# A 32-expert layer on one core: the down weights move from the sync engine's DMA queue to ScalarE's

## The reference, cut to what matters

```python
def hier_moe(h, w_group, w_router, w_gate, w_up, w_down):
    ...                      # 4 groups x 8 experts; a token takes the group with the largest
    ...                      # probability and in it the two experts with the largest
    def expert_block(args):
        xb, e = args
        return (jax.nn.silu(xb @ w_gate[e]) * (xb @ w_up[e])) @ w_down[e]
    ...                      # every token gets the weighted sum of its two experts' rows
```

## Time and profile before

| | us |
|---|---|
| median of 3 runs (1653.45 to 1655.84) | 1654.09 |
| the profiled execution's own time | 1657.84 |
| its span, first to last instruction | 1656.1 |
| TensorE busy in the span | 1534.6 (93%) |
| expert layer in the span, from about 255 to 942 | 687 |

### The profile page before, as it was taken

The page is one execution under the profiler, slowest core; times in us unless marked ns, Lnnn a source line. Parts: engine busy times, 40 slices in busy tenths (PEclk is TensorE's granted clock), DMA queues, the critical chain, the costliest instruction groups (busy, mean ns, idle before and its releaser), DMA issues.

```text
span 1656.1 us, 22332 instructions
## 1 busy us (share of the span) xinstructions
PE 1534.6 (93%) x9534; PEld 1079.2 (65%) x9534; DVE 565.9 (34%) x982; ACT 330.4 (20%) x530; POOL 23.0 (1%) x31
## 2 busy tenths in 40 slices
PE   6997689999999999999999789999789999899996
PEld 4784475444444444444444479999677767799996
DVE  4747632111111110111111175555435263355553
ACT  2202221111111111111111132222200041244441
POOL 0002000000000000000000000000100000000000
PEclk9897888999999999999999999999989999999997
DMA  9870457999999999999999968777386500345440
GB/s 371 342 256 1 174 240 311 428 432 434 433 432 433 431 433 428 432 432 433 433 433 432 376 233 291 261 271 261 104 336 231 201 1 25 129 153 203 173 157 25
DMA packets 124504, 480.32 MB, mean 290 GB/s; under 512 B 6316, under 2 KB 53673, under 8 KB 108081
## 3 DMA queue, kind: packets, MB, share of 16 engines
q1 hardware_dynamic: 120896, 476.99, 71.8%
q10 hardware_dynamic: 3121, 1.18, 0.3%
q0 software_dynamic: 448, 1.59, 0.3%
HBM read 478.68 MB, written 1.06 MB: 290 GB/s over the span
## 4 chain that ended last, share of the span: by engine, by line
PE 71%; DMA 20%; DVE 5%; ACT 2%; ACTq 1%; issue 1%; SPq 0%; DVEq 0%
DMA arena<-in_w_up_dram 18%; PE psum L870 16%; PE psum L1196 16%; PE psum L1123 13%; PE psum L1217 8%; PE psum L1142 5%; PE psum L1107 2%; PE psum L1089 2%; PE psum L886 1%; DMA arena<-in_w_in_dram 1%; PE psum L969 1%; PE psum L1010 1%; PE psum L1021 1%; PE psum L895 1%; PE psum L904 1%
## 5 line engine op out<-in xcount | busy, mean ns | idle before, releaser
L1123 PE MATMUL psum<-arena,squares 128*64 128x384 f32 x2048 | 337.9, 487 | 19.4 <-DMA arena<-in_w_up_dram 14.6
L1123 PEld LDWEIGHTS psum<-arena,squares 128*64 128x64 f32 x2048 | 145.9, 137 | 213.5 <-issue 181.5
L1720 DVE TENSOR_TENSOR mixT<-mixT,psum 128x384 f32<-128x384 f32 x32 | 26.4, 827 | 489.2 <-PE psum L1123 489.2
L870 PE MATMUL psum<-hT,arena 128*128 128x256 f32 (+1 forms) x784 | 174.5, 385 | 11.8 <-DMA arena<-in_w_in_dram 10.3
L870 PEld LDWEIGHTS psum<-hT,arena 128*128 128x128 f32 (+1 forms) x784 | 150.3, 193 | 34.2 <-DMA arena<-in_w_in_dram 10.7
L1142 PE MATMUL psum<-arena,small 128*64 128x512 f32 x768 | 171.9, 597 | 0.0
L1142 PEld LDWEIGHTS psum<-arena,small 128*64 128x64 f32 x768 | 52.4, 137 | 95.9 <-issue 94.0
L1196 PE MATMUL psum<-ff_x_hi,ff_w_hi 128*128 128x256 f32 x704 | 106.4, 293 | 8.8 <-ACT ff_x_hi L678 8.8
L1765 DVE TENSOR_TENSOR ff_w_lo<-arena,ff_w_hi 128x2048 fp32r<-128x2048 f32 x44 | 100.8, 2291 | 16.8 <-ACT ff_w_hi L770 15.3
L1196 PEld LDWEIGHTS psum<-ff_x_hi,ff_w_hi 128*128 128x128 f32 x704 | 93.7, 192 | 12.5 <-issue 9.5
L1382 DVE SCALAR_TENSOR_TENSOR mod_acc<-arena,cond,mod_acc 128x512 f32<-128x512 f32 x133 | 100.0, 752 | 4.7
(11 more groups left out here) (265 smaller groups left out, 1404.2 us busy)
## 6 DMA issues: line engine op xcount, KB each, us to landing
arena<-in_w_gate_dram SPq DMA_DIRECT2D x32, 3072.0 KB, 31.6
arena<-in_w_up_dram SPq DMA_DIRECT2D x32, 3072.0 KB, 33.9
arena<-in_w_down_dram SPq DMA_DIRECT2D x32, 3072.0 KB, 31.6
arena<-in_ffn_w_in_dram SPq DMA_DIRECT2D x44, 1024.0 KB, 7.1
arena<-in_w_ada_dram SPq DMA_DIRECT2D x18, 2048.0 KB, 11.7
arena<-in_w_mod_dram SPq DMA_DIRECT2D x12, 2048.0 KB, 16.2
arena<-in_w_in_dram SPq DMA_DIRECT2D x11, 2048.0 KB, 13.8
arena<-in_ffn_w_out_dram SPq DMA_DIRECT2D x22, 1024.0 KB, 4.8
```

The costliest lines, as they stand in the source:

```text
L870: last = pe.matmul(dst, lhsT=lhs[i], rhs=rhs[i], start=(i == 0), stop=(i == n - 1))
L1123: last = pe.matmul(b[64 * half:64 * half + 64, 0:HALF_E], lhsT=xeT[:, k, u * SLOTS:(u + 1) * SLOTS], rhs=w[:, k, half * HALF_E:(half + 1) ...
L1720: nc.vector.tensor_tensor(hidden.rearrange("q (c p) -> q p c", c=3), gate_act.rearrange("q (p c) -> q p c", c=3), bank[5][:, 0:HALF_E].rea ...
```

## The change

The loop of SyncE no longer waits for `down_done` and no longer requests the down block. ScalarE requests it, on its own queue, right behind its copy of expert e-2's result to `y_e`; its loop is one pair shorter, and the last pair, which has nothing to load behind it, is written out. The down blocks of experts 0 and 1 and the second pass stay with SyncE.

```diff
-            def load_expert(u, e, done):
+            def load_expert(u, e, done, with_down=True):
                 sp.wait_ge(sem("gate_done"), done)
                 load_gate(u, e)
                 sp.wait_ge(sem("gate_up_done"), done)
                 load_up(u, e)
-                sp.wait_ge(sem("down_done"), done)
-                load_down(u, e)
+                if with_down:
+                    sp.wait_ge(sem("down_done"), done)
+                    load_down(u, e)
...
-                    load_expert(u, it * 2 + u, it * 2 + u - 1)
+                    load_expert(u, it * 2 + u, it * 2 + u - 1, with_down=False)
...
+            def next_down(u, e):
+                _, _, down = expert_w(u)
+                act.dma_start(down.rearrange("p (h c) n -> p h c n", h=2),
+                              ins["w_down"][0][bass.ds(e, 1)].rearrange("a (h p c) n -> p (a h) c n", h=2, p=P))\
+                   .then_inc(sem(f"down_full{u}"), 16)
+
             pair_in(1)
-            with act.Fori(0, N_EXPERTS // 2) as it:
+            with act.Fori(0, N_EXPERTS // 2 - 1) as it:
                 for u in range(2):
                     expert_steps(u, it * 2 + u + 1, it + 2)
+                    next_down(u, it * 2 + u + 2)
+            for u in range(2):
+                expert_steps(u, N_EXPERTS - 1 + u, N_EXPERTS // 2 + 1)
```

## The result

The changed kernel takes 1661.01 us (median of 5 runs, 1659.19 to 1662.61) against 1654.09 us: a ratio of 1.0045, 95% interval 1.003 to 1.006. The prediction had 1660.7 us. When it was run again beside the first experiments it took 1661.28 us, a ratio of 1.0043 (1.0029 to 1.0057) to the kernel before. Single executions of some versions were slower at a lower clock than the rest of the same kernel; the ratios leave them out, the medians of the two versions with four transfers for each down block do not.

What follows compares the result with a forecast made beforehand. DMA transfers were taken to bound the expert layer, narrowly ahead of TensorE. Requesters cost 0, arrival order 6.6 us, added to the median 1654.09 for 1660.7 us; range 1652.5 to 1667.

Steps and rivals of the forecast that it cites:

- What bounds the kernel: Expert layer: DMA transfers at 432 GB/s, 43.68 us a pair against TensorE's 40.77; last byte kept at 926.6.
- SyncE and ScalarE at no cost: Expert loop: moving 30 requests of 0.38 us from SyncE to ScalarE costs 0 us, hidden in waits and idle time.
- Packets in turn: DMA engines take one packet from each queue in turn, whatever its size; down blocks get a third of the rate.
- R: Gate and up packets still to come when expert 30's down block is through; taken as 4, end 943.2, 6.6 us late.
- The equal counts and the third of the bytes: Sign in the expert stretch: as many packets of q10 (down blocks) as of q1, with a third of the bytes.
- its bounds: End of the layer: between 3.4 us late (R = 7.5) and 10.2 us late (R = 0).
- the same formula: End of the layer: at or after the later of 946.8 - 0.91 R and 936.6 + 0.455 R.
- a mixing out of step: Sign: if q10, the down blocks' queue, runs dry between blocks, the queues do not mix as written out.
- Waits from 520 on, about 29 us in total: TensorE in the expert layer: waits on even experts' down blocks, starting near 520, about 29 instead of 19 us.
- What follows the layer shifts along: Behind the expert layer: everything moves with its later end; nothing from 972 to 1186 gives time back.
- rival 3: Expert stretch: mixing two streams lowers the DMA rate; one percent less adds 6.5 us, 1667.2 us; chance 0.11.
- no effect: Whole kernel: down packets served in request order or blocks still landing in order of use; 1654.1 us; chance 0.14.
- two queues fill gaps: Stretch from 267 to 926: second queue fills idle moments, each percent 6.5 us; 1647.6 at 2%; chance 0.15.

Runs made afterwards that it cites:

- the run with 90 requests on ScalarE: Changed kernel with SyncE's loop taken out, ScalarE requesting gate, up and down blocks of experts 2 to 31; layer 675.3 us, ratio 1.0015 to the kernel before.
- the run with the short tail: Kernel before, with expert 31's gather for a pair that does not exist cut from 32 matmuls to 4; layer 674.6 us, ratio 1.0009.

## Why the prediction was right, and where it was not

- *What bounds the kernel*: right. The rate held (432 to 433 GB/s with one queue, with two, and with all on ScalarE), and the last byte came 664.9 us after the first gate matmul in both kernels.
- *SyncE and ScalarE at no cost*: right within the 0.5 us of the run with 90 requests on ScalarE. In the changed kernel the request for down 31 goes out at 896.36, TensorE being done with down 29 at 896.2, while the copy ahead of it is still running (896.22, 0.60 us).
- *Packets in turn*: right, by the order of the packets and by the runs with other packet sizes. The equal counts and the third of the bytes, which the prediction named as signs, could not have come out otherwise. Another of its signs reads the result wrongly: waits on up blocks with an end near 943 were to mean shares equal in bytes. The waits were on up blocks and the layer took 682.0 us, which is an end at 943.8 in its terms, and the queues still took packets in turn; R = 16 and equal bytes give the same time, 7.3 us.
- *The step that failed: R*. The prediction took R, the q1 packets still to come when the down block of expert 30 is through, as 4, with all waits on down blocks of even experts and an end 6.6 us late. In the trace down 30 lands at 870.06 + 29.0 = 899.1, up 31 at 920.9: 21.9 us or 16 rounds later. R is 16, the far end of its bounds, where the same formula has 7.3 us; measured are 7.2. The prediction took q10 to have work all the time; it ran dry, which was its own sign for a mixing out of step. What was missing was the turn of the closing packet: the packet records show it, and so does the run with two transfers for each down block. With the turns made equal the waits sit where the prediction put them, and the layer is 6.9 us late.
- *Waits from 520 on, about 29 us in total*: the first is at 525.8, but the list has 17.4 us (18.8 us before). The prediction did not have the clock: behind five of the nine waits the 32 matmuls took 7.07 or 8.35 us instead of 5.38, 9.7 us in total, which would otherwise have been waiting.
- *What follows the layer shifts along*: right; from the end of the down matmuls to the end of the span it is 719.5 us before and 719.2 after.
- *Small slips*: the page has 15 slices of 428 to 434 GB/s in a row, not 14, and rival 3's 1667.2 us lies just outside the 1652.5 to 1667 that is said to take it in. Nothing else rests on either.
- *The rivals*: "no effect" and "two queues fill gaps" fall with the ratio's interval and the unchanged rate; "mixing costs rate" does too, for packets of 12 and 24 KiB. With packets of 4 KiB it does cost, 420 against 429 GB/s.

That the time came out within 0.3 us of the forecast owes something to luck: R = 4 and R = 16 happen to lie on either side of the minimum, 6.6 and 7.3 us late. What carried the forecast were its bounds: with packets of 24 and 12 KiB in turn every R from 0 to 16 ends between 3.4 and 10.2 us late. They don't hold for other packets: with 4 KiB the mixing cost 37.0 us.

## What to carry to other kernels

Where transfers set the pace, as here, one queue in the order of use was not beaten: the second queue added no bandwidth (432 GB/s either way), it only let later blocks overtake those that were wanted next. The order mattered at the end of the loaded stretch (+7.1 us for the second half of the blocks) and not ahead of it (+0.1 us for the first), so look there first: which block is the last one that much work stands behind, and what else is on the engines while it comes. With two queues in use count packets, the closing ones too, and not bytes.

## What the runs showed of the hardware that I had not expected

- The small closing packet of a transfer counts as a turn between the queues: 430 of 432 stood between two packets of the other queue, and one more on each engine moved all of TensorE's waits from up to down blocks (17.4 us on up in the change, 20.5 us on down with two transfers).
- Down blocks in four transfers of 64 partitions each, with packets of 12 KiB as before, moved the mean rate (400 to 900) from 432 to 267 GB/s on one queue and to 272 on two, with the engines at 101% and every kind of packet longer. The cause is open.
- Down blocks in packets of 4 KiB cost 4.8 us on one queue, 429 against 432 GB/s.
- The length of a wait does not tell whether TensorE's clock drops behind it. In the run with the first half of the blocks on ScalarE two waits took 1.94 us each; the 32 matmuls behind the one at 786.83 took 5.38 us, behind the one at 874.25 they took 7.07. Behind the last wait it was 5.38 us in the kernel before (granted clock 1.00, wait of 1.89 us) and 7.07 in the run with the short tail (0.76, wait of 1.97 us). At this one place, behind the last block, the difference of 1.7 us is paid in full.
